# Up projections of two feed-forwards: seven half-size products a group in place of eight

## The chip, the cores and the metric

The kernel runs on 1 core of one Trainium2 chip. The metric is the device time of one execution in microseconds (us); the median of three runs of the kernel before is 2188.79 us (2188.71 to 2190.12). A time is compared with the kernel before on the same chip.

## The reference

A network of three layers over 256 tokens of 1024 channels, all in float32: two layers with a mixer, cross-attention to a memory and a gated feed-forward, then a layer with attention, a recurrence and 32 experts. The change lies in the two gated feed-forwards:

```python
def conv_glu_ffn(xn, w_up, conv_w, conv_b, w_down):
    u, gt = split_cols(xn @ w_up, (D_FF, D_FF))      # D_FF = 2752, w_up is 1024 x 5504
    u = causal_dwconv(u, conv_w, conv_b)             # 3 taps along the tokens
    return (jax.nn.silu(u) * gt) @ w_down
...
h = h + conv_glu_ffn(rms_norm(h, norm_ffn_g[layer]), ffn_w_up[layer], ffn_conv_w[layer],
                     ffn_conv_b[layer], ffn_w_down[layer])
```

## The kernel before

**Lanes.** The program is written once for each engine: a lane object (P for TensorE, V for VectorE, S for ScalarE, G for GpSimd, F for SyncE's DMA queue) issues in the order of the code. `mark` names the last instruction of a lane, `wait_ge` waits for such names. Each VectorE or ScalarE instruction also waits for the one before it on its engine. So each engine's order is written out by hand, and an instruction that waits holds all behind it.

**Layout.** Activations have channels on the 128 partitions and tokens on the free axis: `XT` is 8 blocks of 128 channels by 256 tokens. Weights are the stationary operand. `P.mm` (line 412 of the profile) on float32 shows in the profile as two LDWEIGHTS and two MATMUL. PSUM has 8 banks of 128 x 512; `P.tile` takes the next of banks 0 to 3, `P.occupy` a named one, and both wait until its last user is freed (`V.free`).

**Loads.** `LOADS` (line 195) is the order in which F issues the weight units of 2 MB into a ring of 4 slots of 4096 columns in feed-forward 0 and 5 in feed-forward 1 (line 591). A slot is loaded again once the unit in it was reported with `P.used`; at most 4 loads are in flight. Units `up0.g` and `up1.g` are the groups of the up projections, `dn` the down projection, `ada` the modulation weights that VectorE multiplies out behind each feed-forward.

**The feed-forward** (`ffn_p`, `ffn_s`, `ffn_v`, lines 2295 to 2390). The 2752 columns of u and of the gate are cut into 11 groups of 256 (the last has 192). For a full group TensorE fills two banks, one with u and one with the gate, each two tiles of 128 channels by 256 tokens, each tile 8 `mm` of 256 columns: 32 `mm` a group. In the last group the 64-wide tiles of u and gate are paired on the two halves of the array (`halves`). The rows that enter are not yet divided by their root mean square: ScalarE writes `XT` = gain x h and the squares as the layer before ends, TensorE adds the squares up after the first bank (`added_p`), ScalarE and VectorE make the root (`root_s`, `root_v`), which VectorE multiplies onto each bank as it takes it from PSUM. Then VectorE makes the causal convolution (per tile one multiply-add at line 323 and two at line 329), ScalarE the Silu, VectorE the product into `AC`, which the down projection reads. The down projection (`down_p`) adds 21 blocks and a half block into banks 4 to 7, in passes of 4 blocks, the last groups together in its last pass. Behind the last group VectorE works off the next mixer's small sums and the `ada` units beside the down projection.

```python
def added_p(P, n):
    b = P.tile(n + ".ss")
    P.wait_ge(f"{n}.qs")
    for c in range(2):
        P.mm(b[:, 0:256], ONESD, SQ[:, c, :], c == 0, c == 1, sig=n + ".ss" if c else None)
```

## Time and profile before

| | |
|---|---|
| median of 3 runs | 2188.79 us (2188.71 to 2190.12) |
| the profiled execution: own time, span | 2190.6 us, 2188.7 us |
| mean granted TensorE clock | 0.978 |
| busy: PE, PEld, DVE, ACT, POOL | 2057.1, 1372.6, 618.3, 367.0, 111.2 us |
| DMA | 587.77 MB, mean 269 GB/s |
| up projections of the two feed-forwards | from 359.34 and from 826.68 us after the span's start |

PE is TensorE's matmuls, PEld its weight loads, DVE VectorE, ACT ScalarE, POOL GpSimd, SPq the DMA queue of SyncE. A row of the timeline gives the start and the busy time in us, the engine, the line, the operation, output <- inputs with shapes, and xcount; in brackets the idle time before it and what ended it. Forms are rows by shape: busy us in all and mean ns of one.

### The profile page before, as it was taken

The page shows a single profiled execution, that of the slowest core. Times are in us where ns is not written, and L with a number is a line of the kernel's source. Part 1 is how long each engine was busy: PE and PEld are TensorE (multiplying, and loading weights), DVE is VectorE, ACT ScalarE, POOL GpSimd, SP SyncE. Part 2 cuts the span into 40 slices and gives each one's busy share as a digit, 9 for nine tenths or more (in the row PEclk, how much of TensorE's full clock was granted, in tenths as well). Part 3 has the DMA queues.
Part 4 walks back from the last instruction along what each step waited for, and adds up shares of the span by engine and source line. Part 5 has one row for each costly group of instructions (what it writes and reads, how often), then busy time and mean ns, then how long its engine had stood idle before and what let it go on. Part 6 is the DMA issues. An engine that isn't in the chain of part 4 may idle for free.

```text
span 2188.7 us, 27681 instructions
## 1 busy us (share of the span) xinstructions
PE 2057.1 (94%) x11650; PEld 1372.6 (63%) x11650; DVE 618.3 (28%) x1258; ACT 367.0 (17%) x706; POOL 111.2 (5%) x186
## 2 busy tenths in 40 slices
PE   9999999999999999999999999977699999898976
PEld 6888788888888888888777733322243333333423
DVE  5445432335364133344334321100011111101101
ACT  4322132000042121000232410100000100000101
POOL 0123100000000000000000000100000000001000
PEclk9999999999999999999999999988899999999987
DMA  7221343435524445348433499999999999999996
GB/s 269 107 78 41 155 174 116 154 144 222 212 82 154 154 163 220 141 159 332 174 132 130 183 381 426 427 427 427 427 426 411 427 427 427 427 427 428 420 427 283
DMA packets 44581, 587.77 MB, mean 269 GB/s; under 512 B 5393, under 2 KB 5665, under 8 KB 9505
## 3 DMA queue, kind: packets, MB, share of 16 engines
q1 hardware_dynamic: 44448, 585.92, 65.9%
q8 instruction: 94, 1.54, 0.3%
q14 instruction: 39, 0.31, 0.0%
HBM read 584.85 MB, written 1.05 MB: 268 GB/s over the span
## 4 chain that ended last, share of the span: by engine, by line
PE 69%; DMA 28%; ACT 1%; DVE 1%; issue 1%; SPq 0%; ACTq 0%; DVEq 0%
PE pb L412 68%; DMA ring<-in_gu 16%; DMA ring<-in_dne 9%; DMA arena<-in_dne 2%; PE pb L422 1%; DMA arena<-in_gu 1%; ACT arena L373 0%; DVE arena L329 0%; DMA xs<-in_rw_g 0%; DVE arena L323 0%; ACT arena L379 0%; SPq L591 0%; DVE ring L314 0%; DVE arena L314 0%; ACT xs L373 0%
## 5 line engine op out<-in xcount | busy, mean ns | idle before, releaser
L412 PE MATMUL pb<-arena,ring 128*128 128x256 f32 (+2 forms) x2784 | 605.8, 382 | 2.1 <-ACT arena L373 2.0
L412 PEld LDWEIGHTS pb<-arena,ring 128*128 128x128 f32 (+2 forms) x2784 | 519.1, 189 | 80.5 <-issue 7.5
L412 PE MATMUL pb<-arena 64*64 64x64 f32 (+12 forms) x3084 | 401.0, 342 | 19.8 <-DMA arena<-in_dne 10.5
L412 PEld LDWEIGHTS pb<-arena 64*64 64x64 f32 (+5 forms) x3084 | 280.9, 155 | 126.0 <-issue 94.1
L412 PE MATMUL pb<-arena,cst 128*64 128x512 f32 (+6 forms) x1108 | 275.4, 612 | 41.5 <-DMA ring<-in_gu 41.0
L412 PE MATMUL pb<-ring,cst 128*64 128x512 f32 (+2 forms) x784 | 246.9, 626 | 7.2 <-DMA arena<-in_gu 3.9
L412 PEld LDWEIGHTS pb<-arena,cst 128*64 128x64 f32 (+4 forms) x1108 | 88.8, 140 | 196.2 <-issue 193.9
L412 PE MATMUL pb<-ring,arena 128*64 128x512 f32 (+4 forms) x608 | 157.6, 536 | 8.0 <-DMA arena<-in_dne 6.3
L321 DVE TENSOR_SCALAR arena<-pb 128x512 f32<-128x512 f32 x30 | 20.7, 691 | 463.6 <-PE pb L412 463.6
L379 ACT ACTIVATE arena<-pb 128x512 f32<-128x512 f32 (+2 forms) x128 | 65.8, 514 | 490.2 <-PE pb L422 393.6
L373 ACT ACTIVATE arena<-arena 128x512 f32<-128x512 f32 (+6 forms) x151 | 87.7, 581 | 310.8 <-DVE arena L329 271.0
L314 DVE TENSOR_TENSOR arena<-pb,arena 128x512 f32<-128x512 f32 (+6 forms) x127 | 64.6, 509 | 223.6 <-PE pb L412 210.2
L412 PEld LDWEIGHTS pb<-ring,cst 128*64 128x64 f32 (+2 forms) x784 | 73.9, 139 | 77.1 <-issue 77.1
L323 DVE TENSOR_SCALAR arena<-pb 128x512 f32<-128x512 f32 x30 | 20.7, 691 | 333.6 <-PE pb L412 333.6
L412 PE MATMUL pb<-kv,cst 128*64 128x512 f32 (+2 forms) x240 | 110.6, 616 | 1.7 <-DMA ring<-in_gu 1.7
L412 PE MATMUL pb<-kv,arena 128*64 128x512 f32 (+4 forms) x288 | 95.4, 485 | 16.2 <-DMA arena<-in_dne 10.5
L412 PEld LDWEIGHTS pb<-ring,arena 128*64 128x64 f32 (+3 forms) x608 | 59.4, 140 | 55.9 <-issue 55.0
L314 DVE TENSOR_TENSOR arena<-arena 128x512 f32<-128x512 f32 (+6 forms) x134 | 79.0, 590 | 28.2 <-ACT arena L373 17.9
L379 ACT ACTIVATE memt<-pb 128x512 f32<-128x512 f32 (+1 forms) x39 | 22.0, 564 | 374.2 <-PE pb L412 374.0
L412 PE MATMUL pb<-arena,kv 128*128 128x256 f32 (+1 forms) x384 | 82.1, 381 | 1.2 <-ACT arena L379 1.2
L412 PEld LDWEIGHTS pb<-kv,arena 128*128 128x128 f32 (+2 forms) x288 | 42.7, 152 | 63.4 <-issue 61.9
L412 PEld LDWEIGHTS pb<-arena,kv 128*128 128x128 f32 (+1 forms) x384 | 68.8, 186 | 12.3 <-ACT arena L379 1.6
(149 smaller groups left out, 1479.8 us busy)
## 6 DMA issues: line engine op xcount, KB each, us to landing
arena<-in_gu SPq DMA_DIRECT2D x64, 2048.0 KB, 19.4
ring<-in_gu SPq DMA_DIRECT2D x49, 2048.0 KB, 19.4
arena<-in_dne SPq DMA_DIRECT2D x30, 2048.0 KB, 19.4
ring<-in_dne SPq DMA_DIRECT2D x22, 2048.0 KB, 19.4
kv<-in_gu SPq DMA_DIRECT2D x15, 2048.0 KB, 19.4
ring<-in_up SPq DMA_DIRECT2D x13, 2048.0 KB, 7.8
ring<-in_ada SPq DMA_DIRECT2D x8, 2048.0 KB, 7.8
kv<-in_dne SPq DMA_DIRECT2D x8, 2048.0 KB, 19.3
```

The lines of the kernel that those rows point to most:

```text
L314: self.e.tensor_tensor(out, a, b, op).then_inc(self.sem, 1)
L321: self.e.tensor_scalar(out, a, s1, None, op0).then_inc(self.sem, 1)
L323: self.e.tensor_scalar(out, a, s1, s2, op0, op1).then_inc(self.sem, 1)
L373: self.e.activation(out, a, func, bias=bias, scale=scale, accum_out=accum).then_inc(self.sem, 1)
L379: self.e.activation(out, a, ACT.Copy).then_inc(self.sem, 1)
L412: r = self.e.matmul(out, lhsT, rhs, start=start, stop=stop, skip_group_check=True)
L422: r = self.e.transpose(out, a, ident)
```

## The change

Each of the ten full groups of an up projection is a product of 2 x 2 blocks: the rows split in halves of tokens (i) and in even and odd channel blocks (e), `XA[i][e]`, the weights by e and by u or gate, `corners`. It is made with seven block products and sums (Winograd's form of Strassen's method) in place of eight. A block product is 8 `mm` of 128 columns into half a bank.

- The last, narrow group is done first, in the form that it had, on unscaled rows. Then VectorE scales the rows in place (`halved_v`) and makes four sums of them, once for each feed-forward.
- For each group VectorE makes four sums of weight blocks, 128 x 1024 elements each (`weight_sums_v`; t3 in place in the ring slot, the others in spare memory, two sets), in general one group ahead.
- TensorE runs P1, P6, P5, P7, P2, P4, P3 (`seven_p`); P2 is added onto P1 and P3 onto P5 in PSUM, after ScalarE has copied P1 out (`first`) and VectorE has read P5 (`c22`). In group 0 P2 comes second and has a bank of its own. Groups alternate between banks 0 to 3 and 4 to 7.
- VectorE combines: U2 = P1 + P6, U3 = U2 + P7, gate of the second tokens U3 + P5, u of them U3 - P4, gate of the first U2 + P5 + P3; u of the first is P1 + P2, copied by ScalarE. The convolution, Silu and product of a group are made while the next one is multiplied; its multiply with bias moves to ScalarE (`tap`).
- `LOADS` has the last group's unit first.

```diff
 LOADS = """
 ab_small ab.0 ab.1 ab.2 ab_r.1 ab_r.0 ab_r.2 rw_scratch wkv0.0 wkv0.1 wkv0.2 wkv0.3 mixo0.0 mixo0.1 wq0.0
-wq0.1 wo0.0 wo0.1 up0.0 up0.1 up0.2 up0.3 up0.4 up0.5 up0.6 up0.7 up0.8 up0.9 up0.10 dn0.0 ada.0 dn0.1 ada.1
+wq0.1 wo0.0 wo0.1 up0.10 up0.0 up0.1 up0.2 up0.3 up0.4 up0.5 up0.6 up0.7 up0.8 up0.9 dn0.0 ada.0 dn0.1 ada.1
...
-mixo1.1 wq1.0 wq1.1 wo1.0 ada.4 wo1.1 ada.5 up1.0 up1.1 up1.2 up1.3 up1.4 up1.5 up1.6 up1.7 up1.8 up1.9 up1.10
+mixo1.1 wq1.0 wq1.1 wo1.0 ada.4 wo1.1 ada.5 up1.10 up1.0 up1.1 up1.2 up1.3 up1.4 up1.5 up1.6 up1.7 up1.8 up1.9
...
+        XT4 = XT_.rearrange("p (q e t) -> p q e t", q=4, e=2)
+        XA = [[XT4[:, :, e, i * 128:(i + 1) * 128] for e in range(2)] for i in range(2)]
+        XSUM = MX_.rearrange("p (s q t) -> p s q t", s=4, q=4)
+        FIRST, U2, U3 = (XS_[:, o:o + 256].rearrange("p (j t) -> p j t", j=2) for o in (512, 768, 1024))
+        def corners(w):
+            q = w.rearrange("p (q e n) -> p q e n", q=4, e=2)
+            return [[q[:, :, e, h * 256:(h + 1) * 256] for h in range(2)] for e in range(2)]
+        def halved_v(V, n, after):
+            V.wait_ge(*after)
+            for i, e in ((0, 0), (0, 1), (1, 0), (1, 1)):
+                V.tt(XA[i][e], XA[i][e], bc(RB[:, i * 128:(i + 1) * 128], 1, 4), MUL)
+                V.mark(f"{n}.a{i}{e}")
+            s1, s2, s3, s4 = (XSUM[:, k] for k in range(4))
+            V.tt(s1, XA[1][0], XA[1][1], ADD)
+            V.tt(s2, s1, XA[0][0], SUB)
+            V.mark(f"{n}.s2")
+            V.tt(s3, XA[0][0], XA[1][0], SUB)
+            V.mark(f"{n}.s3")
+            V.tt(s4, XA[0][1], s2, SUB)
+            V.mark(f"{n}.s4")
+        def weight_sums_v(V, unit, spare, which, after=None):
+            b = corners(V.unit(unit)[:, 0:4096])
+            t1, t2, t4 = spare
+            if 1 in which:
+                if after is not None:
+                    V.wait_ge(after)
+                V.tt(t1, b[0][1], b[0][0], SUB)
+                V.tt(t2, b[1][1], t1, SUB)
+                V.mark(f"{unit}.t2")
+            if 3 in which:
+                V.tt(b[0][1], b[1][1], b[0][1], SUB)
+                V.mark(f"{unit}.t3")
+            if 4 in which:
+                V.tt(t4, t2, b[1][0], SUB)
+                V.mark(f"{unit}.t4")
+        def seven_p(P, unit, n, xn, spare, k0, first):
+            b = corners(P.unit(unit)[:, 0:4096])
+            t1, t2, t4 = spare
+            s1, s2, s3, s4 = (XSUM[:, k] for k in range(4))
+            def product(bank, lhs, rhs, sig, start=True):
+                for j in range(2):
+                    for q in range(4):
+                        P.mm(bank[:, j * 128:(j + 1) * 128], lhs[:, q, j * 128:(j + 1) * 128], rhs[:, q, :],
+                             start and j + q == 0, q == 3, sig=sig if (j, q) == (1, 3) else None)
+            one = P.occupy(f"{n}a", k0)
+            P.wait_ge(f"{xn}.a00")
+            product(one, b[0][0], XA[0][0], f"{n}.p1")
+            if first:
+                three = P.occupy(f"{n}f", 3)
+                P.wait_ge(f"{xn}.a01")
+                product(three, b[1][0], XA[0][1], f"{n}.p2")
+            six = P.occupy(f"{n}b", k0 + 1)
+            P.wait_ge(f"{xn}.s2", f"{unit}.t2")
+            product(six, t2, s2, f"{n}.p6")
+            five = P.occupy(f"{n}d", k0 + 2)
+            product(five, t1, s1, f"{n}.p5")
+            seven = P.occupy(f"{n}c", k0 + 3)
+            P.wait_ge(f"{xn}.s3", f"{unit}.t3")
+            product(seven, b[0][1], s3, f"{n}.p7")
+            if not first:
+                P.wait_ge(f"{n}.first")
+                product(one, b[1][0], XA[0][1], f"{n}.p2", start=False)
+            four = P.occupy(f"{n}e", k0 + 1)
+            P.wait_ge(f"{xn}.a11", f"{unit}.t4")
+            product(four, t4, XA[1][1], f"{n}.p4")
+            P.wait_ge(f"{xn}.s4", f"{n}.c22")
+            product(five, b[1][1], s4, f"{n}.p3", start=False)
             P.used(unit)
...
+        UG = XS_[:, 1536:2048].rearrange("p (q t) -> p q t", q=2)
+        SEVENS, LAST = 10, 10
+        quarter = lambda t, *at: [t[:, o:o + 1024].rearrange("p (q n) -> p q n", q=4) for o in at]
+        SPARE = [[quarter(KV_, 0, 1024, 2048), quarter(AR.t, 10752, 11776, 13312)],
+                 [quarter(AR.t, 8192, 9216, 10240), quarter(AR.t, 11264, 12288, 13312)]]
+        def first_bank(g):
+            return 4 - 4 * (g % 2)
         def ffn_p(P, n):
             P.begin(f"ffn{n}")
...
-            for g, (w2, tiles) in enumerate(FFN):
-                w = P.unit(f"up{n}.{g}")[:, 0:16 * w2].rearrange("p (k n) -> p k n", k=8)
-                names = [f"{f}.u{g}", f"{f}.g{g}"]
-                bs = [P.tile(name, hold=True) for name in names]
-                for b, name, c0 in zip(bs, names, (0, w2)):
-                    for q, (c1, cw) in enumerate(tiles):
-                        if cw < 128:
-                            if c0 == 0:
-                                halves(w, b, w2, c1, name)
-                            continue
-                        for c in range(8):
-                            P.wait_ge(f"{f}.x{c // 2}")
-                            P.mm(b[0:cw, q * 256:(q + 1) * 256], w[:, c, c0 + c1:c0 + c1 + cw], XT[:, c, :], c == 0,
-                                 c == 7, sig=name if (c == 7 and (q == 1 or (c0 and tiles[1][1] < 128))) else None)
-                    if g == 0 and c0 == 0:
...
+            w2, tiles = FFN[LAST]
+            P.main, P.i = [2], 0
+            w = P.unit(f"up{n}.{LAST}")[:, 0:16 * w2].rearrange("p (k n) -> p k n", k=8)
+            names = [f"{f}.u{LAST}", f"{f}.g{LAST}"]
+            for name, c0 in zip(names, (0, w2)):
+                b = P.occupy(name, 1 if c0 else 0)
+                for c in range(8):
+                    P.wait_ge(f"{f}.x{c // 2}")
+                    P.mm(b[:, 0:256], w[:, c, c0:c0 + 128], XT[:, c, :], c == 0, c == 7, sig=name if c0 and c == 7 else None)
+                if c0 == 0:
+                    halves(w, b, w2, 128, name)
+                    added_p(P, f)
+            P.used(f"up{n}.{LAST}")
+            for g in range(SEVENS):
+                seven_p(P, f"up{n}.{g}", f"{f}.{g}", f, SPARE[n][g % 2], first_bank(g), g == 0)
+            P.main, P.i = [0, 1, 2, 3], 0
             down_p(P, FBLOCKS, f"dn{n}", 4, f"dn{n}", ready=lambda kk: f"{f}.ac{kk}", merged=2,
                    halves=FHALF)
...
             root_s(S, f)
-            for g, (w2, tiles) in enumerate(FFN):
-                S.reach(f"{f}.g{g}")
-                cb = CB2[g % 2]
+            def tap(g):
+                S.wait_ge(f"{f}.u{g}.in")
+                for q, (c1, cw) in enumerate(FFN[g][1]):
...
+                    S.act(CB2[g % 2][0:cw, q, :], UB[0:cw, q, :], ACT.Identity,
...
+                S.mark(f"{f}.tap{g}")
+            def silu(g):
                 S.wait_ge(f"{f}.c{g}")
-                for q, (c1, cw) in enumerate(tiles):
-                    S.act(cb[0:cw, q, :], cb[0:cw, q, :], ACT.Silu)
+                for q, (c1, cw) in enumerate(FFN[g][1]):
+                    S.act(CB2[g % 2][0:cw, q, :], CB2[g % 2][0:cw, q, :], ACT.Silu)
                     S.mark(f"{f}.s{g}{q}")
+            def first(g):
+                S.wait_ge(f"{f}.{g}.p1")
+                if g:
+                    S.wait_ge(f"{f}.{g - 1}.u2" if g > 1 else f"{f}.0.c11")
+                S.copy(FIRST, tokens_half(S.banks[first_bank(g)]))
+                S.mark(f"{f}.{g}.first")
+            def copied(g):
+                S.wait_ge(f"{f}.{g}.p2", f"{f}.c{g - 1}")
+                S.copy(UB[:, :, 0:128], tokens_half(S.banks[first_bank(g)]))
+                S.free(f"{f}.{g}a")
+                S.mark(f"{f}.{g}.c11")
+            first(0)
+            S.free(f"{f}.0a")
+            tap(LAST)
+            silu(LAST)
+            tap(0)
+            for g in range(1, SEVENS):
+                first(g)
+                silu(g - 1)
+                copied(g)
+                tap(g)
+            silu(SEVENS - 1)
             S.table(LNEXP)
+            def conv(g):
+                V.wait_ge(f"{f}.tap{g}")
+                for q, (c1, cw) in enumerate(FFN[g][1]):
+                    cb, u = CB2[g % 2][0:cw, q, :], UB[0:cw, q, :]
+                    for k in (1, 0):
+                        o, late = coff["fcw"] + n * 66 + 22 * k + g * 2 + q, 2 - k
+                        V.stt(cb[:, late:256], u[:, 0:256 - late], COL[0:cw, o:o + 1], cb[:, late:256], MUL, ADD)
+                V.mark(f"{f}.c{g}")
+            def gated(g):
+                for q, (c1, cw) in enumerate(FFN[g][1]):
+                    V.wait_ge(f"{f}.s{g}{q}")
+                    cb, at = CB2[g % 2][0:cw, q, :], g * 2 + q
+                    V.tt(AC[0:cw, at, :], UG[0:cw, q, :], cb, MUL)
+                    if cw == 64:
+                        V.tt(AC[64:128, at, :], UG[0:cw, q, :], cb, MUL)
+                    V.mark(f"{f}.ac{at}")
+            def sums(g, *which):
+                if g < SEVENS:
+                    weight_sums_v(V, f"up{n}.{g}", SPARE[n][g % 2], which, f"used up{n}.{g - 2}" if g > 1 else None)
+            def last_in():
+                b = V.got(f"{f}.u{LAST}")
+                V.tt(UB[:, 0, :], b[:, 0:256], RB, MUL)
+                V.tt(UB[0:64, 1, :], b[0:64, 256:512], RB[0:64], MUL)
+                V.mark(f"{f}.u{LAST}.in")
+                V.tt(UG[0:64, 1, :], b[64:128, 256:512], RB[64:128], MUL)
+                V.free(f"{f}.u{LAST}")
+                b = V.got(f"{f}.g{LAST}")
+                V.tt(UG[:, 0, :], b[:, 0:256], RB, MUL)
+                V.free(f"{f}.g{LAST}")
             root_v(V, f)
...
+            sums(0, 1, 3, 4)
+            halved_v(V, f, (f"{f}.u{LAST}", f"{f}.g{LAST}"))
+            for g in range(SEVENS):
+                m, before = f"{f}.{g}", g - 1 if g else LAST
+                one, six, five, seven = (tokens_half(V.banks[first_bank(g) + k]) for k in range(4))
+                if g:
+                    sums(g + 1, 1)
+                V.wait_ge(f"{m}.first", f"{m}.p6")
+                V.tt(U2, FIRST, six, ADD)
+                V.mark(f"{m}.u2")
+                V.free(f"{m}b")
+                if g == 0:
+                    V.wait_ge(f"{m}.p2")
+                    last_in()
+                    sums(1, 1)
+                conv(before)
+                if g == 0:
+                    V.tt(UB[:, :, 0:128], FIRST, tokens_half(V.banks[3]), ADD)
+                    V.free(f"{m}f")
+                    V.mark(f"{m}.c11")
+                sums(g + 1, 3)
+                V.wait_ge(f"{m}.p7")
+                V.tt(U3, U2, seven, ADD)
+                V.free(f"{m}c")
+                gated(before)
+                V.wait_ge(f"{m}.p5")
+                V.tt(UG[:, :, 128:256], U3, five, ADD)
+                V.mark(f"{m}.c22")
+                sums(g + 1, 4)
+                V.wait_ge(f"{m}.p4")
+                if g:
+                    V.wait_ge(f"{m}.c11")
+                V.tt(UB[:, :, 128:256], U3, six, SUB)
+                V.free(f"{m}e")
+                V.mark(f"{f}.u{g}.in")
+                V.wait_ge(f"{m}.p3")
+                V.tt(UG[:, :, 0:128], U2, five, ADD)
+                V.free(f"{m}d")
+            conv(SEVENS - 1)
+            gated(SEVENS - 1)
...
                 if what in ("up0", "up1"):
-                    return [(0, 128, flat(what, 128, 16 * FFN[int(n)][0]))]
+                    at, size = (128 * 16 * sum(f[0] for f in FFN[k0:k1]) for k0, k1 in ((0, int(n)), (int(n), int(n) + 1)))
+                    return [(0, 128, dram[what][at:at + size].rearrange("(p n) -> p n", p=128))]
```

## Rows read from the trace of the kernel before

**Rows 1.** The page: chain that ended last by engine, and landing of loads.
```profile
PE 69%; DMA 28%; ACT 1%; DVE 1%; issue 1%; SPq 0%; ACTq 0%; DVEq 0%
...
ring<-in_up SPq DMA_DIRECT2D x13, 2048.0 KB, 7.8
```

**Rows 2.** The chain in order of time: start, length, what.
```profile
318.70 0.87 PE pb L422 x8
...
328.19 263.45 PE pb L412 x1240
...
795.52 259.14 PE pb L412 x1220
```

**Rows 3.** Stretches: both up projections, then one full group.
```profile
core 0: us, PE busy (x) PEld busy (x) DVE busy (x) ACT busy (x) POOL busy (x), PEclk, DMA share, GB/s
359.34:508.95 149.61, 149.61 (x709) 130.84 (x708) 57.04 (x115) 12.15 (x26) 0.00 (x0) 1.00 0.41 151
826.68:976.28 149.60, 149.60 (x709) 130.85 (x708) 57.04 (x115) 12.15 (x26) 0.00 (x0) 1.00 0.44 165
374.02:387.83 13.81, 13.81 (x65) 12.19 (x64) 4.99 (x10) 1.08 (x3) 0.00 (x0) 1.00 0.40 152
```

**Rows 4.** Timeline of PE in the expert part: 128 columns each, then what follows.
```profile
1283.03 3.74 PE L412 MATMUL pb<-arena,xs 128*128 128x128 f32 x32
1286.61 0.38 PE L422 MATMUL pb<-cst,arena 128*128 128x128 f32 x2
```

**Rows 5.** Timeline, feed-forward 0, weight loads of the last group: halves, then gate.
```profile
501.88 3.22 PEld L412 LDWEIGHTS pb<-arena,ring 128*64 128x64 f32 x32 [0.33 <-issue]
505.49 58.57 PEld L412 LDWEIGHTS pb<-arena,ring 128*128 128x128 f32 x272 [0.38 <-issue]
```

**Rows 6.** Timeline at the start of feed-forward 0.
```profile
359.34 7.07 PE L412 MATMUL pb<-arena 128*128 128x256 f32 x32
...
366.25 1.03 PE L412 MATMUL pb<-xs,small 128*128 128x256 f32 x4
...
367.31 0.47 ACT L373 ACTIVATE arena<-pb,small 128x256 f32<-128x256 f32 x1 [5.33 <-PE pb L412]
...
368.32 0.42 DVE L329 SCALAR_TENSOR_TENSOR arena<-pb,arena 128x256 f32<-128x256 f32 x1 [5.62 <-ACT arena L373]
...
369.70 0.69 DVE L314 TENSOR_TENSOR arena<-pb,arena 128x512 f32<-128x512 f32 x1
...
370.88 1.01 DVE L329 SCALAR_TENSOR_TENSOR arena<-arena,col 128x255 f32<-128x255 f32 x2
...
373.40 0.86 ACT L373 ACTIVATE arena<-arena 128x256 f32<-128x256 f32 x2 [3.81 <-DVE arena L329]
```

**Rows 7.** Timeline of DVE in two other places: sums of 1024 elements.
```profile
110.10 2.06 DVE L314 TENSOR_TENSOR arena<-arena 128x1024 f32<-128x1024 f32 x1
...
1148.00 3.75 DVE L314 TENSOR_TENSOR arena<-arena 128x1024 f32<-128x1024 f32 x3
```

**Rows 8.** Groups of DVE by form, whole span: 512 elements, 256 elements.
```profile
L314 DVE TENSOR_TENSOR arena<-arena 128x512 f32<-128x512 f32 x52 | 36.0, 692 | 4.4 <-DVE arena L329 0.5
...
L314 DVE TENSOR_TENSOR arena<-pb,arena 128x256 f32<-128x256 f32 x44 | 18.7, 425 | 31.7 <-PE pb L412 29.1
```

**Rows 9.** Stretches of 1 us around an idle PE, columns as in rows 3.
```profile
1057.00:1058.00 1.00, 0.31 (x2) 0.00 (x0) 0.93 (x3) 0.00 (x0) 0.00 (x0) 1.00 1.04 442
1058.00:1059.00 1.00, 0.00 (x0) 0.00 (x0) 0.93 (x3) 0.85 (x2) 0.00 (x0) 1.00 1.00 426
1059.00:1060.00 1.00, 0.69 (x3) 0.67 (x4) 0.93 (x3) 0.88 (x3) 0.00 (x0) 0.96 0.99 426
1060.00:1061.00 1.00, 1.00 (x4) 0.61 (x4) 0.93 (x3) 0.88 (x3) 0.00 (x0) 0.50 1.03 442
...
1063.00:1064.00 1.00, 1.00 (x5) 0.84 (x5) 0.30 (x1) 0.57 (x2) 0.00 (x0) 0.83 0.00 0
```

More of the change, by code:

```diff
@@ L831, in proj_tok_p @@
                          sig=f"{n}{i}" if c == 7 else None)
+            P.used(unit)
+        XT4 = XT_.rearrange("p (q e t) -> p q e t", q=4, e=2)
[5 more added lines that the diff above has]
+            return [[q[:, :, e, h * 256:(h + 1) * 256] for h in range(2)] for e in range(2)]
@@ new lines, in tokens_half @@
+        def tokens_half(bank):
+            return bank[:, 0:256].rearrange("p (j t) -> p j t", j=2)
+        def seven_p(P, unit, n, xn, spare, k0, first):
[30 more added lines that the diff above has]
+            product(five, b[1][1], s4, f"{n}.p3", start=False)
@@ L2304, in halves @@
                          sig=name if c == 7 else None)
-            for g, (w2, tiles) in enumerate(FFN):
-                w = P.unit(f"up{n}.{g}")[:, 0:16 * w2].rearrange("p (k n) -> p k n", k=8)
-                names = [f"{f}.u{g}", f"{f}.g{g}"]
-                bs = [P.tile(name, hold=True) for name in names]
-                for b, name, c0 in zip(bs, names, (0, w2)):
-                    for q, (c1, cw) in enumerate(tiles):
-                        if cw < 128:
-                            if c0 == 0:
-                                halves(w, b, w2, c1, name)
-                            continue
-                        for c in range(8):
-                            P.wait_ge(f"{f}.x{c // 2}")
-                            P.mm(b[0:cw, q * 256:(q + 1) * 256], w[:, c, c0 + c1:c0 + c1 + cw], XT[:, c, :], c == 0,
-                                 c == 7, sig=name if (c == 7 and (q == 1 or (c0 and tiles[1][1] < 128))) else None)
-                    if g == 0 and c0 == 0:
-                        added_p(P, f)
-                P.used(f"up{n}.{g}")
-                for name in names:
-                    P.release(name)
+            w2, tiles = FFN[LAST]
[14 more added lines that the diff above has]
+            P.main, P.i = [0, 1, 2, 3], 0
             down_p(P, FBLOCKS, f"dn{n}", 4, f"dn{n}", ready=lambda kk: f"{f}.ac{kk}", merged=2,
@@ L2347, in ffn_v @@
             added_v(V, f)
-            root_v(V, f)
-            def fc(name, at, cw):
-                o = coff[name] + at
-                return COL[0:cw, o:o + 1]
-            def normed(b, tiles):
-                if len(tiles) == 2 and tiles[1][1] == 128:
-                    V.tt(UB, pair(b), bc(RB, 1, 2), MUL)
-                else:
-                    for q, (c1, cw) in enumerate(tiles):
-                        V.tt(UB[0:cw, q, :], b[0:cw, q * 256:(q + 1) * 256], RB[0:cw], MUL)
-            for g, (w2, tiles) in enumerate(FFN):
-                cb = CB2[g % 2]
-                ub = [UB[0:cw, q, :] for q, (_, cw) in enumerate(tiles)]
-                b = V.tile(f"{f}.u{g}")
-                normed(b, tiles)
-                if tiles[1][1] == 64:
-                    ub[1] = CB2[1 - g % 2][0:64, 1, :]
-                    V.tt(ub[1], b[64:128, 256:512], RB[64:128], MUL)
-                V.free(f"{f}.u{g}")
-                for q, (c1, cw) in enumerate(tiles):
-                    jj = g * 2 + q
-                    conv_v(V, cb[0:cw, q, :], UB[0:cw, q, :],
-                           [fc("fcw", n * 66 + 22 * k + jj, cw) for k in range(3)], fc("fcb", n * 22 + jj, cw))
-                V.mark(f"{f}.c{g}")
-                normed(V.tile(f"{f}.g{g}"), [t for t in tiles if t[1] == 128])
-                V.free(f"{f}.g{g}")
-                for q, (c1, cw) in enumerate(tiles):
-                    V.wait_ge(f"{f}.s{g}{q}")
-                    V.tt(AC[0:cw, g * 2 + q, :], ub[q], cb[0:cw, q, :], MUL)
-                    if cw == 64:
-                        V.tt(AC[64:128, g * 2 + q, :], ub[q], cb[0:cw, q, :], MUL)
-                    V.mark(f"{f}.ac{g * 2 + q}")
```

4 lines of the change are left out of this document (added).

## The prediction

> **What bounds the kernel.** I read the page's chain first: TensorE (PE) makes 69% of it, the DMA engines 28% [rows 1]. Then the chain in order of time, to see which share the two feed-forwards have: each lies inside one unbroken PE piece of about 260 us [rows 2], so neither loads nor other engines end a wait there, and a microsecond of PE saved there, or of PE idleness added, moves everything behind it, the loads of the expert part too, as their slots are freed by PE. Then the stretches of the up projections: 149.6 us each, PE busy for all of it at granted clock 1.00, VectorE (DVE) for 57.0, ScalarE (ACT) for 12.2, GpSimd for nothing, and a full group costs 13.81 us [rows 3]. The kernel's `mm` on f32 shows as two MATMULs, so a group's 32 products are 64 instructions of 0.2158 us. DVE has 8.8 us to spare in each group. The question is what the new order asks of DVE, and when.
>
> **Removed and added on PE.** A full group becomes seven products of 8 `mm` with 128 columns in place of 32 with 256: 7 x 16 = 112 MATMULs. Columns fall to 7/8, but each instruction is only 128 columns long and each takes new weights. The nearest rows: 32 such matmuls start at 1283.03 and the next at 1286.61, 0.1119 us each; runs of 8 transposes of the same shape take 0.87 us, 0.1088 each [rows 4]. I take 0.1117, since a product stream is long like the first: 1.79 us a product, 12.51 a group, 1.30 less than before. Ten groups and two feed-forwards: **-26.0 us**; at 0.1088 it would be 32.5. (The Trainium skill, TensorE: Matmul & The Clock Gate, "Wait — 56ns, not 53.3ns?", gives a fixed 2.5 ns per matmul over the column time. The 0.2158 us here agree, taken as two passes; for 128 columns that makes an estimate of 0.1092, so the gain would be 5.6 us more; the long run says 0.0025 more per instruction.)
>
> **The last group goes first**, on unscaled rows, with bank and work unchanged: first product 3.45 us, the halves 3.61 (501.88 to 505.49 [rows 5]), the sum of squares 0.86, gates 3.45. It only moves, at no cost.
>
> **First new wait: rows and weight sums before group 0.** At feed-forward 0, PE starts at 359.34 [rows 6]. The sum of squares is then issued by 359.34 + 3.45 + 3.61 = 366.40 (before: 366.25), and PE ends the last group at 366.40 + 0.86 + 3.45 = 370.7. DVE has the root at 369.70 + 0.15 = 369.85 [rows 6]. Its queue then holds the four weight sums of group 0 (`sums(0, 1, 3, 4)`, 1024 elements each): three such operations take 3.75 us in a row [rows 7], 1.26 each with the gap, so 5.04, until 374.9. Only then come the scaled rows, 512 elements each: 0.69 [rows 8], until 375.6, and PE begins P1 at about 375.65. **PE idle 5.0 us.** P1 and P2 (3.6 us) then just cover the other three scalings and s1, s2 (5 x 0.73 = 3.65): 0.1 us more.
>
> **Second new wait: C22 of group 0.** P6, P5, P7, P4 follow, until 375.65 + 6 x 1.79 + 0.1 = 386.45. P3 adds into the bank of P5, so it waits for `c22`. DVE gets P6 at 381.3 and has these ahead of `c22`, in its own order: U2 (256 elements from PSUM, 0.425 [rows 8], 0.465 with the gap), the four of `last_in` 1.85, `sums(1,1)` 2.52, the convolution of the last group 2.08 (1.01 for two of four [rows 6]), C11 0.46, `sums(1,3)` 1.26, U3 0.46, three of `gated` 1.4, C22 0.42: 10.9 us, until 392.3. ACT's Silu (0.86 for two [rows 6]) fits beside `sums(1,3)`. **PE idle 5.9 us.** P3 ends at 394.1.
>
> **Steady state.** From group 1 the weight sums run a group ahead. Count from PE's start of a group: DVE ends the last UG of the group before at 0.7, `sums(g+1,1)` at 3.2, waits for P6 (3.57 + 0.2), U2 at 4.25, the convolution at 6.3, `sums(g+1,3)` at 7.6, U3 at 8.1, `gated` at 9.0, C22 at 9.5. PE reaches P3 at 10.7: covered with 1.2 us over. The fourth sum ends at 10.75, before P4 is done (10.9). DVE is busy 10.4 of 12.5 us (4 x 1.26, 5 + 2 of 0.465, 2.08). Loads: a slot is filled again a group's length after it is free, and a load of `up` lands 7.8 us after its issue [rows 1]; DVE asks for a group's weights one group sooner than PE did, still about 25 us after the issue. Cost nothing, in all three. The units that follow `up` are asked for one place later in the ring, 2 MB in 12.5 us. The last scalar table, Silu and tail of DVE lie behind the down projection, whose first passes need only early groups.
>
> Without the clock, one up projection: 11.4 (last group and sum) + 4.95 + 10.8 + 5.85 + 1.8 + 9 x 12.51 = 147.4 against 11.4 + 10 x 13.81 = 149.5 us, twice: **-4.2 us**.
>
> **The clock.** The nearest idle stretch of PE is the one at 1057.3 to 1059.3, 2.0 us: then the granted clock was 0.50 for about 3.4 us of work (1060 to 1063.4) and 1.00 again [rows 9]. At 0.50 (1.2 in place of 2.4 GHz) that costs half of 3.4 us, 1.7. My idle stretches are longer (5.0, 5.9), so each should bring it; part of the slow stretch may fall into the idle one, and it can come twice. Bounds per wait: 0 and 3.4; I take 1.5, near the one row. Four waits: **+6.0 us**. In the first pair it delays P6 and with it `c22`, so nothing hides it. (The Trainium skill, the same page, "Loop structure matters more than you think": long waits between bursts of matmuls take the clock back to its lower level. The row at 1060 agrees. By that rule all four waits pay, by the -4.2 alone none does.)
>
> **Sum**: -26.0 + 21.8 (both waits and the 0.1, twice) + 6.0 = +1.8 us. The profiled execution took 2190.6 us, 1.8 more than the median 2188.8; I add the change to the median: **2190.6**. Under 0.2% (4.4 us) a measurement here can't tell from no change.
>
> **The rivals.**
> (1) *The PE stream is faster than I take it, or the clock stays up.* 0.1088 us per matmul gives 2190.6 - 6.5 = 2184.1; with no clock drop as well, 2178. For it: the 8-runs [rows 4]. Against: the 32-run, and the row of the clock. By the Trainium skill's figure alone, in place of 0.1117, it would be 2185.0.
> (2) *Slower: VectorE's `c22` comes late in every group.* Place: P3's wait; slack 1.2 us. Ahead of it stand three sums and nine smaller operations since the wait at the group's start, so it decides once they take 0.1 us more each. A 128x1024 sum did take 2.06 us where GpSimd worked beside it [rows 7]: three at +0.8 less the slack are 1.2 us, in 18 groups 22 us, so 2212; half of that, 2201. Against: GpSimd does nothing in these stretches [rows 3].
> (3) *Slower: the half clock comes twice after each wait*, 3.4 us each: -4.2 + 13.6 gives 2198.2. The row shows it once after 2.0 us; nothing shows it for 5 to 6.
> (4) The change doesn't give the seventh it names: this is in my sum (1.30 of 13.81 us, 9%, not 12.5%).
>
> **Chances.** Forecast 0.55; (1) 0.17; (2) 0.13; (3) 0.15. All of the forecast's own range, 2186.5 to 2193, is within 0.2%; (1) is faster, (2) and (3) slower. The range goes from 2181.5 (most of 1) to 2201 (3 and the mild form of 2).
>
> **What would show it.** Two PE idle stretches per feed-forward, released by VectorE, of about 5.0 us (before the first 128-column product) and 5.9 (ahead of the seventh product of group 0), and none after; clock rows of 0.50 behind each; groups of 12.5 us by windows; each up projection 147.4 us plus the clock's part, 150 to 151; 128x1024 sums at 1.23 us; nothing changed in length after 509 or before 359. Wrong if a PE wait recurs in each group, if groups take 12.2 us, or if the idle stretches are shorter since the sums are not in the way.

## The result, and the profile after

| | before | after |
|---|---|---|
| median | 2188.75 us (2188.64 to 2190.12, 4 runs) | 2205.33 us (2204.82 to 2207.88, 4 runs) |
| the profiled execution: own time, span | 2190.6 us, 2188.7 us | 2205.69 us, 2203.9 us |
| mean granted TensorE clock | 0.978 | 0.971 |
| first up projection, from the span's start | 359.34 to 508.95 us | 370.95 to 523.15 us |
| second up projection | 826.68 to 976.28 us | 840.95 to 993.88 us |

The ratio is 1.0076, 95% interval 1.0064 to 1.0088: 16.6 us slower by the medians, 15.2 by the two spans. The forecast was 2190.6, at most 2201.0.

First the page of after, the chain that ended last; it answers to [rows 1].

```profile
PE 67%; DMA 28%; DVE 3%; ACT 1%; issue 1%; SPq 0%; DVEq 0%; ACTq 0%
PE pb L412 66%; DMA ring<-in_gu 9%; DMA kv<-in_gu 6%; DMA kv<-in_dne 4%; DMA ring<-in_dne 3%; DMA arena<-in_gu 3%; DMA arena<-in_dne 2%; DVE arena L314 1%; PE pb L422 1%; ACT arena L373 1%; DVE arena L329 1%; DMA arena<-in_cond 0%; DMA xs<-in_rw_g 0%; DVE ring L314 0%; DVE kv L314 0%
```

VectorE's share rose from 1 to 3%, and there is a link that the chain before did not have: a load of `in_cond`. Nothing in the up projections reads it.

The stretches of after: both up projections, then a steady group; columns as in [rows 3], to which they answer.

```profile
370.95:523.15 152.20, 141.24 (x1189) 138.11 (x1188) 109.52 (x170) 32.56 (x67) 0.00 (x0) 0.97 0.41 153
840.95:993.88 152.93, 141.97 (x1189) 138.84 (x1188) 109.54 (x170) 32.53 (x67) 0.00 (x0) 0.96 0.45 169
423.10:435.61 12.51, 12.51 (x115) 12.51 (x113) 9.78 (x15) 2.81 (x7) 0.00 (x0) 1.00 0.45 170
```

A group takes 12.51 us, as forecast to the hundredth; PE idles for 10.96 us in each up projection (152.20 - 141.24), and the clock is under 1.00 in both. Yet these stretches hold only 2.59 + 3.33 = 5.9 of the 15.2 us. The first begins 11.61 us late, so most of the loss lies **ahead** of the changed code. From the end of the second to the end of the span after needs 1210.0 us, 2.4 less than before, in code that wasn't touched. 11.61 + 2.59 + 0.07 (between the two) + 3.33 - 2.4 = 15.2.

SyncE's own timeline in after, ahead of feed-forward 0 (start, length, line, load):

```profile
273.74 14.14 SPq L591 DMA_DIRECT2D ring<-in_wo  x2
302.23 0.33 SPq L591 DMA_DIRECT2D arena<-in_up  x1
302.61 0.42 SPq L600 DMA_DIRECT2D arena<-in_cond  x1
```

and the same place before:

```profile
272.97 14.14 SPq L591 DMA_DIRECT2D ring<-in_wo  x2
287.16 0.42 SPq L600 DMA_DIRECT2D arena<-in_cond  x1
...
301.46 0.33 SPq L591 DMA_DIRECT2D arena<-in_up  x1
```

Before, the small load of `cond` was issued at 287.16, ahead of the first `up` unit, which then waited on the queue for its ring slot until 301.46. After, the two stand the other way round, and `cond` is issued at 302.61. SyncE's lane says why: its fetches are tied to a unit by name, and that unit is no longer the first of its kind.

```python
for name in LOADS.split():
    ...
    if name == "up0.0":
        F.wait_ge("mixo0.a3")
        F.get("cond", CROW, dram["cond"].partition_broadcast(128))
        ...
    F.load(name, *block(name))
```

Who waits for it, in the timeline of after, all engines (in brackets the idle time and what ended it):

```profile
310.60 3.23 ACT L373 ACTIVATE arena<-arena 128x1024 f32<-128x1024 f32 x3 [14.34 <-DMA arena<-in_cond]
313.86 1.22 DVE L314 TENSOR_TENSOR arena<-arena 128x1024 f32<-128x1024 f32 x1 [16.17 <-ACT arena L373]
...
316.75 6.65 PE L412 MATMUL pb<-kv,arena 128*128 128x256 f32 x16 [7.64 <-DVE arena L314]
```

and the stretch at the half clock (granted 0.50, that is 1.2 GHz in place of 2.4), columns as in [rows 3]:

```profile
312.50:322.80 10.30, 6.05 (x14) 4.88 (x15) 4.16 (x6) 2.42 (x6) 0.00 (x0) 0.50 0.00 0
```

ScalarE waits 14.34 us for `cond`, VectorE for ScalarE, and VectorE's next work is what TensorE's attention scores need. Before, the same ScalarE work started at 295.78 after a wait of 0.30 us, and the scores at 308.17. They now come 8.58 us later; 0.77 of this is older (SyncE was already 0.77 late at 273.74, and the last section has the wait that made it), so 7.8, and half of the 6.05 us of matmuls at the half clock is 3.0 more: **10.8 us** before feed-forward 0 starts.

Then the two forecast waits, in the timeline of after, PE and DVE:

```profile
381.73 1.23 DVE L314 TENSOR_TENSOR kv<-ring 128x1024 f32<-128x1024 f32 x1
382.99 1.23 DVE L314 TENSOR_TENSOR kv<-ring,kv 128x1024 f32<-128x1024 f32 x1
384.25 1.23 DVE L314 TENSOR_TENSOR ring<-ring 128x1024 f32<-128x1024 f32 x1
385.51 1.23 DVE L314 TENSOR_TENSOR kv<-kv,ring 128x1024 f32<-128x1024 f32 x1
386.84 5.77 DVE L314 TENSOR_TENSOR arena<-arena 128x512 f32<-128x512 f32 x8
387.68 5.40 PE L412 MATMUL pb<-arena,ring 128*128 128x128 f32 x32 [4.99 <-DVE arena L314]
...
406.19 6.35 PE L412 MATMUL pb<-arena,ring 128*128 128x128 f32 x32 [5.96 <-DVE xs L314]
```

Four weight sums, then the rows, and PE has idled 4.99 us; then 5.96 us for `c22`. Feed-forward 1 shows 4.99 and 5.97, and no other PE wait of an up projection stands in the trace. The 32 matmuls behind each wait take 5.40 and 6.35 us where others take 3.74: the half clock. In the stretches behind the waits it is:

```profile
388.00:389.00 1.00, 1.00 (x6) 1.00 (x6) 0.95 (x2) 0.00 (x0) 0.00 (x0) 0.50 1.03 442
...
405.00:407.00 2.00, 0.81 (x4) 0.81 (x5) 1.90 (x4) 0.00 (x0) 0.00 (x0) 0.50 0.00 0
407.00:409.00 2.00, 2.00 (x11) 2.00 (x11) 0.81 (x2) 1.01 (x2) 0.00 (x0) 0.50 0.03 8
409.00:411.00 2.00, 2.00 (x11) 2.00 (x11) 0.89 (x2) 0.19 (x1) 0.00 (x0) 0.50 0.17 33
```

It lasts from 387.6 to 391.0 and from 404.7 to 411.5, in feed-forward 1 from 855.2 to 862.1 and from 875.7 to 882.5. The matmul work in the four is 3.3, 5.3, 4.5 and 5.9 us; half of it is lost: 1.65 + 2.65 + 2.25 + 2.95 = **9.5 us** in place of the 6.0 of the forecast.

### The profile page after: what moved, and what is told of

The parts are those of the page before. It is cut to its first block, busy times and chain, and to the rows that moved or that the text cites. A ratio compares the mean times of both kernels' runs of the same rounds, so it can differ in the third digit from the quotient of the medians.

```text
span 2203.9 us, 29905 instructions
## 1 busy us (share of the span) xinstructions
PE 2043.0 (93%) x12610; PEld 1388.1 (63%) x12610; DVE 724.4 (33%) x1372; ACT 408.0 (19%) x788; POOL 111.2 (5%) x186
## 3 DMA queue, kind: packets, MB, share of 16 engines
q8 instruction: 101, 1.65, 0.3%
## 4 chain that ended last, share of the span: by engine, by line
PE 67%; DMA 28%; DVE 3%; ACT 1%; issue 1%; SPq 0%; DVEq 0%; ACTq 0%
PE pb L412 66%; DMA ring<-in_gu 9%; DMA kv<-in_gu 6%; DMA kv<-in_dne 4%; DMA ring<-in_dne 3%; DMA arena<-in_gu 3%; DMA arena<-in_dne 2%; DVE arena L314 1%; PE pb L422 1%; ACT arena L373 1%; DVE arena L329 1%; DMA arena<-in_cond 0%; DMA xs<-in_rw_g 0%; DVE ring L314 0%; DVE kv L314 0%
## 5 line engine op out<-in xcount | busy, mean ns | idle before, releaser
L412 PE MATMUL pb<-arena,ring 128*128 128x256 f32 (+3 forms) x2816 | 527.8, 350 | 13.1 <-DVE xs L314 6.0
L412 PEld LDWEIGHTS pb<-arena,ring 128*128 128x128 f32 (+2 forms) x2816 | 461.9, 192 | 70.8 <-issue 12.6
L412 PE MATMUL pb<-arena 128*128 128x128 f32 (+14 forms) x3804 | 454.3, 322 | 19.4 <-DMA arena<-in_dne 10.3
L412 PEld LDWEIGHTS pb<-arena 128*128 128x128 f32 (+5 forms) x3804 | 340.2, 162 | 118.4 <-issue 92.6
L412 PE MATMUL pb<-ring,cst 128*64 128x512 f32 (+2 forms) x784 | 247.4, 625 | 10.2 <-DMA arena<-in_gu 3.9
L373 ACT ACTIVATE arena<-arena 128x512 f32<-128x512 f32 (+5 forms) x151 | 87.7, 581 | 145.2 <-DVE arena L329 90.9
L412 PE MATMUL pb<-arena,kv 128*128 128x128 f32 (+2 forms) x592 | 97.8, 325 | 12.1 <-DVE xs L314 6.0
L314 DVE TENSOR_TENSOR arena<-arena 128x512 f32<-128x512 f32 (+5 forms) x120 | 90.2, 751 | 39.4 <-ACT arena L373 32.6
L412 PEld LDWEIGHTS pb<-arena,kv 128*128 128x128 f32 (+1 forms) x592 | 86.8, 200 | 18.8 <-DVE xs L314 6.2
L412 PE MATMUL pb<-memt,arena 128*128 128x512 f32 (+3 forms) x204 | 70.6, 504 | 1.2 <-ACT memt L379 1.2
L314 DVE TENSOR_TENSOR ht<-pb,ht 128x512 f32<-128x512 f32 x24 | 16.6, 691 | 163.6 <-PE pb L412 163.6
```

Source lines behind the costliest of these rows:

```text
L314: self.e.tensor_tensor(out, a, b, op).then_inc(self.sem, 1)
L373: self.e.activation(out, a, func, bias=bias, scale=scale, accum_out=accum).then_inc(self.sem, 1)
L412: r = self.e.matmul(out, lhsT, rhs, start=start, stop=stop, skip_group_check=True)
```

## The experiments

Each is compared with the kernel before on the same chip; a median is one of 4 to 10 runs.

**The load's place alone.** e1_cond_first is after with the fetches ahead of the first `up` unit again; e2_before_cond_late is the kernel before with only the fetches moved behind its first `up` unit.

```diff
 # e1, on after
-                if name == "up0.0":
+                if name == "up0.10":
 # e2, on before
-                if name == "up0.0":
+                if name == "up0.1":
```

> The changed kernel with one line different: the DMA queue fetches the condition vector and the gate weights ahead of up0.10 (as it did ahead of up0.0 before the change), not behind it. Theory (queue): up0.10 waits on SyncE for its ring slot until about 302 us, cond is issued 15 us later than before, ScalarE stands before it in cross-attention 0 and PE with it; with the line moved, cond is issued near 287 us again, the PE idle stretch of 7.6 us and the half clock of 10.2 us behind it go, feed-forward 0 starts near 359 to 360 us, and the time falls by 10.8 us from 2205.3 to about 2194.5. Rival (the loss lies elsewhere, in the ring's rotation or the clock): the idle stretch before feed-forward 0 stays or comes back in another place, and the time stays within 3 us of 2205.

> The kernel before, with nothing of the seven products: only cond and the gate weights are fetched behind the first up unit in place of ahead of it. Theory (queue): the same idle stretch of 7 to 8 us before the keys' scores of cross-attention 0, half clock behind it, +10.8 us: 2188.8 to about 2199.6. Rival (the wait belongs to the new products or to the new order of groups): no change, 2188.8.

Measured: e1 2196.04 us (2193.62 to 2197.34), ratio 1.0028 [1.0017, 1.0039]; e2 2199.49 us (2198.8 to 2201.26), ratio 1.0046 [1.003, 1.0063]. The timeline of PE in e2, a kernel without any of the seven products, and its half clock (columns as in [rows 3]):

```profile
317.06 5.45 PE L412 MATMUL pb<-kv,arena 128*128 128x256 f32 x16 [8.47 <-DVE arena L314]
```
```profile
313.80:320.60 6.80, 3.54 (x8) 2.86 (x9) 3.30 (x4) 0.34 (x1) 0.00 (x0) 0.50 0.00 0
```

8.47 + 3.54 / 2 = 10.2 us, and the median rose by 9.9 against the runs of before beside it. In e1 there is no PE wait there, and the loss against before falls from 16.6 to 6.4 us (2196.04 - 2189.62), so by 10.2. The order of two loads is worth 10 us and the rest of the change 6.4: shown from both sides. The stretch of feed-forward 1, where the edit touches nothing, is 152.90 us in e1 and was 152.93 in after.

**The clock apart from the waits.** e5_warm_in_waits is e1 with TensorE kept at work in its two waits, on products that nobody reads; VectorE's order, and so the time at which PE may go on, is unchanged.

```diff
+            if first:
+                for _ in range(11):
+                    P.mm(one[:, 256:512], ident, cst["tri"], True, True)
             P.wait_ge(f"{xn}.a00")
...
+            if first:
+                idle = P.occupy(f"{n}w", 2)
+                for _ in range(13):
+                    P.mm(idle[:, 256:512], ident, cst["tri"], True, True)
+                P.free(f"{n}w")
             P.wait_ge(f"{xn}.s4", f"{n}.c22")
```

> e1 with 11 and 13 matmuls of 256 columns whose result nobody reads, put ahead of PE's two waits of group 0 in each feed-forward (4.7 and 5.6 us of work in waits of 5.0 and 6.0). Theory (the clock's price is what the -4.2 us lack): the granted clock stays at 1.00 through both up projections, each is about 147.5 us long, and the time falls from 2194.5 by about 9.5 us to 2185. Rival (half clock costs nothing that isn't in the waits already, something else makes the up projections 152 to 153 us): 2194 or more.

Measured: 2187.87 us (2184.58 to 2191.52, 10 runs), ratio 0.9991 [0.9981, 1.0]. Feed-forward 1 in e1 and in e5, stretches with columns as in [rows 3]:

```profile
828.67:981.57 152.90, 141.94 (x1189) 138.82 (x1188) 109.55 (x170) 32.56 (x67) 0.00 (x0) 0.96 0.45 170
```
```profile
827.67:975.81 148.14, 147.64 (x1237) 143.04 (x1236) 109.54 (x170) 32.58 (x67) 0.00 (x0) 1.00 0.47 175
```

The waits are filled, nothing is computed sooner, and the up projection is 4.76 us shorter at a clock of 1.00. By the medians the clock behind four waits was worth 8.2 us, where 9.5 were expected. The time came out 2.9 above what was expected, 1.5 of it because e1 itself lay that much above its own; 10 runs spread over 6.9 us, and the profiled one lost 3 us before the changed code (the last section shows where).

**The first wait.** e3_sums_early is e1 with the weight sums of group 0 ahead of the root, in a gap of VectorE.

```diff
-            root_v(V, f)
-            sums(0, 1, 3, 4)
+            sums(0, 1, 3, 4)
+            root_v(V, f)
```

> e1 with the four weight sums of group 0 issued on VectorE before the root, where VectorE stands idle for 5.6 us, not behind it. Theory (VectorE's order makes the first wait): the idle stretch of 4.99 us falls to about 0.9 us in each feed-forward (root at 369.9, last group's PE done at 370.9 in the old count, scaling 0.7), the half clock behind it goes too (1.7 to 2.3 us each): 2194.5 to about 2182.5. The second wait stays at 5.9 to 6.0. Rival (the wait is for the scaled rows or the load of up0.0, not for the sums): 4 us or more of idle stay, 2194.

Measured: 2182.29 us (2181.65 to 2183.81), ratio 0.9966 [0.9954, 0.9979]. The timeline of PE in e3, feed-forward 0:

```profile
372.02 3.81 PE L412 MATMUL pb<-arena,ring 128*128 128x128 f32 x32 [0.88 <-DVE arena L314]
...
389.00 5.43 PE L412 MATMUL pb<-arena,ring 128*128 128x128 f32 x32 [5.97 <-DVE xs L314]
```

The first wait shrank from 4.99 to 0.88 us and no half clock follows it (3.81 us for 32 matmuls); the second stayed at 5.97 with its half clock. One line moved turned a kernel 6.4 us slower than before into one 7.3 us faster, 13.8 us where 12 were expected.

**The slack at `c22`.** The forecast had 1.2 us of it in a steady group, from a count of VectorE's queue. e7_two_more_sums is e1 with the first sum of each group computed three times over: 2.5 us more of VectorE work ahead of `c22`.

```diff
-                V.tt(t1, b[0][1], b[0][0], SUB)
+                for _ in range(3):
+                    V.tt(t1, b[0][1], b[0][0], SUB)
```

> e1 with the first weight sum of every group made three times over, 2 x 1.26 us more on VectorE ahead of c22, results unchanged. Theory (steady state has 1.2 us of slack at c22, and PE alone paces it): each of groups 1 to 8 shows a new PE idle stretch of about 1.3 us and lasts 13.8 us in place of 12.51; the two waits of group 0 grow by 2.5 us each: per feed-forward 10.4 + 5.0 us, from 2196.0 to about 2227, up to 2232 with more half clock behind the longer waits. Rival A (VectorE has 2.1 us free in 12.5 wherever it falls, so only 0.4 us a group is lost): groups of 12.9 us, 2212. Rival B (no slack now): groups of 15 us, 2247.

Measured: 2222.81 us (2221.11 to 2223.85), ratio 1.0153 [1.0135, 1.0172]. The timeline of PE in e7: both waits of group 0, then those of groups 1 to 3.

```profile
378.04 6.56 PE L412 MATMUL pb<-arena,ring 128*128 128x128 f32 x32 [7.51 <-DVE arena L314]
...
400.23 5.77 PE L412 MATMUL pb<-arena,ring 128*128 128x128 f32 x32 [8.48 <-DVE xs L314]
...
415.55 3.84 PE L412 MATMUL pb<-arena,ring 128*128 128x128 f32 x32 [0.62 <-DVE xs L314]
...
429.15 2.05 PE L412 MATMUL pb<-arena,ring 128*128 128x128 f32 x16 [0.83 <-DVE xs L314]
...
442.75 2.05 PE L412 MATMUL pb<-arena 128*128 128x128 f32 x16 [0.83 <-DVE xs L314]
```

Now a wait recurs in each of the groups 1 to 8: 0.62 us in the first, then 0.83. From P3 to P3 a group takes 13.60 us (429.15 to 442.75), 1.09 more than 12.51, where the theory had 13.8. How much slack there was stands in the steady group of after that begins at 423.10, in the timelines of DVE (U2, then `c22`) and of PE (P3):

```profile
426.93 0.42 DVE L314 TENSOR_TENSOR xs<-xs,pb 128x256 f32<-128x256 f32 x1 [0.62 <-PE pb L412]
...
432.30 0.42 DVE L314 TENSOR_TENSOR xs<-xs,pb 128x256 f32<-128x256 f32 x1
```
```profile
433.82 1.95 PE L412 MATMUL pb<-arena,ring 128*128 128x128 f32 x16
```

`c22` is done at 432.72 and P3 begins at 433.82: 1.1 us of slack, so the count of 1.2 was right. But VectorE also waits 0.62 us for P6 ahead of U2, and in e7 that wait is gone. Of the 2.52 us of added work it takes 0.62 and the slack 1.10; 0.8 is left, and PE waits 0.83. The recorded count has this wait for P6 too (from 3.2 to 3.77 us), but the theory of e7 left it out. Rival 2 was real as a mechanism and 1.7 us of VectorE work away.

**The second wait, two ways.** e4_group0_order is e3 with VectorE's order in group 0 changed: the last group's rows are taken in before U2, and the sums of group 1 stand behind `c22`. e6_sums_ahead puts the sums of group 0 ahead of the residual of cross-attention, those of group 1 ahead of the root, and keeps the last group's gate in `AC`, so that `c22` need not wait for that group's convolution, Silu and product.

```diff
 # e4, group 0
+                    last_in()
                 V.wait_ge(f"{m}.first", f"{m}.p6")
...
-                    sums(1, 1)
...
-                sums(g + 1, 3)
+                if g:
+                    sums(g + 1, 3)
...
                 V.mark(f"{m}.c22")
-                sums(g + 1, 4)
+                if g:
+                    sums(g + 1, 4)
...
+                if g == 0:
+                    sums(1, 1, 3)
 # e6
+            V.wait_ge(f"{x}.o3")
+            weight_sums_v(V, f"up{n}.0", SPARE[n][0], (1, 3, 4))
             residual_v(V, f"wo{n}")
...
+            sums(1, 1, 3, 4)
             root_v(V, f)
-            sums(0, 1, 3, 4)
...
-                V.tt(UG[:, 0, :], b[:, 0:256], RB, MUL)
+                V.tt(AC[:, 20, :], b[:, 0:256], RB, MUL)
```

> e3 with VectorE's order in group 0 changed: the last group's intake (last_in) comes while P6 runs, and the weight sums of group 1 (sums 1, 3, 4) come behind c22, not ahead of it. Theory (c22 waits for what stands ahead of it in VectorE's queue): the second idle stretch falls from 5.96 to about 1.6 us; the sums put off come back as one stretch of about 1.5 us ahead of P3 of group 1; the half clock behind the second wait (1.7 and 2.2 us in e3) goes. Per feed-forward 2.9 + 1.95 us: from 2182.3 to about 2172.6. Rival (P3 waits for the PSUM bank or for P5's sum itself, not for the queue): the stretch stays at 6 us and the time at 2182.

> The version that should beat both: e1 with the weight sums of group 0 made before the residual of cross-attention, where VectorE waits 22.8 us for PE, those of group 1 before the root, and the last group's gate kept in its own place (AC) so that c22 need not wait for the last group's convolution, Silu and product. Theory: one idle stretch of 0.9 us per feed-forward is left (last group's end to the scaled rows), none at c22, granted clock 1.00, each up projection 137.5 to 138 us against 149.6: 24 us under the kernel before, about 2165.5 beside 2189.6. Rival (VectorE's work of 10.4 us in 12.5 has no room for the backlog at the start, stretches come back in group 1 or 2): 2170 or more.

Measured: e4 2175.8 us (2173.01 to 2179.8), ratio 0.9943 [0.9925, 0.9961]; e6 2175.04 us (2173.82 to 2178.49), ratio 0.9938 [0.992, 0.9956]. e4 has waits of 0.88, 1.44 and 1.91 us in each up projection, and the clock stays at 1.00 through all (141.68 us, feed-forward 1). e6 missed its 2165.5 by 9.5 us. Its feed-forward 0 was nearly as meant (138.4 us, with one wait of 0.34 in group 1); most of the loss stands ahead of feed-forward 1, in the timeline of e6, all engines:

```profile
811.85 1.22 DVE L314 TENSOR_TENSOR arena<-kv 128x1024 f32<-128x1024 f32 x1 [20.54 <-DMA kv<-in_up]
...
816.96 3.08 DVE L314 TENSOR_TENSOR ht<-pb,ht 128x512 f32<-128x512 f32 x4
817.68 1.05 ACT L373 ACTIVATE arena<-ht,col 128x256 f32<-128x256 f32 x2 [30.51 <-DVE ht L314]
...
818.87 4.64 PE L412 MATMUL pb<-arena,ring 128*128 128x256 f32 x12 [4.71 <-ACT arena L373]
...
824.19 4.73 PE L412 MATMUL pb<-arena,ring 128*128 128x256 f32 x36 [0.67 <-ACT arena L373]
```

VectorE waited 20.54 us for the load of `up1.0`, with the residual queued behind it, and PE lost 4.71 and 0.67 us, with 3.4 us at the half clock (818.4 to 821.8) behind the first. It is a queue's order again: an instruction moved ahead on its engine to where its load is not there yet holds all behind it.

**Both put together.** e8_sums_behind_c22 is e6 without the early sums in feed-forward 1, and with the weight sums of the next group behind `c22` in every group.

```diff
-            weight_sums_v(V, f"up{n}.0", SPARE[n][0], (1, 3, 4))
+            if n == 0:
+                weight_sums_v(V, f"up{n}.0", SPARE[n][0], (1, 3, 4))
...
-            sums(1, 1, 3, 4)
+            sums(n ^ 1, 1, 3, 4)
             root_v(V, f)
...
                 V.mark(f"{m}.c22")
+                if g or n:
+                    sums(g + 1, 1)
```

(turns 3 and 4 of the sums follow the mark of u and the last UG in the same way; their places ahead of `c22` go.)

> The run e6_sums_ahead with two edits. In feed-forward 1 no weight sum stands ahead of the residual any more (there VectorE was late for the next load and PE waited 4.71 and 0.67 us, with 3.4 us at the half clock behind them); the sums of group 0 stand ahead of the root and those of group 1 behind c22. And in every group the three turns of weight sums for the next group stand behind c22 instead of ahead of it. Theory (every wait left in e6 is VectorE's order): 2175.0 - 4.7 - 0.7 - 1.7 - 0.7 (the 0.34 of group 1, twice) = 2167.3 us; feed-forward 1 begins near 814.7 without a wait ahead of it, each up projection takes 138.0 us, groups 12.51 us each, the granted clock is 1.00 throughout both. Rival 1 (the sums now come late for the next group: t3 or t4 ends 1.8 us into it, and P6 or P7 waits for them): a PE wait of 0.5 to 1 us recurs in each group, 2175 to 2185 us. Rival 2 (the sums of group 1 are late in feed-forward 1 alone, as in e4_group0_order): 2 to 3.4 us more there, 2169.5 to 2171.

Measured: **2167.07 us** (2165.61 to 2168.12, 4 runs), ratio 0.99 [0.9884, 0.9917] against 2189.45 us for before: 22.4 us faster. Both up projections, stretches of e8:

```profile
359.18:497.19 138.01, 137.13 (x1190) 134.21 (x1189) 104.67 (x167) 32.66 (x67) 0.00 (x0) 1.00 0.45 168
813.00:952.68 139.68, 137.44 (x1189) 134.16 (x1188) 109.58 (x170) 32.55 (x67) 0.00 (x0) 1.00 0.50 185
```

The first is what was expected, 138.0; in the second rival 2 of that run holds in a mild form, PE waits of 0.60 and 0.77 us for group 1's sums and `c22`. The total still met the theory because the second began at 813.0, not at 814.7. Against 149.6 us before, 21.5 us are gained here, of the 26.0 that the products alone bring. Between the two up projections this profiled execution is another 1.9 us shorter than before's (315.8 against 317.7), most of which is not the change's doing: before's has 3.4 us of half clock there, in code that is the same in both, and this one has none (the last section).

## Why the prediction was wrong

**The step that failed** stands under "Steady state": the loads were to "Cost nothing, in all three", and the last part staked "nothing changed in length after 509 or before 359". I asked when each unit is asked for and whether its slot is free; I did not ask what else is in SyncE's lane between the units, and so left this queue at nothing. The unit moved to the front of `LOADS` passed the fetches of `cond` and the gates, whose place hangs on the name `up0.0`, and SyncE held them for 14.7 us (302.61 - 287.16, less the 0.77) while it waited for a slot. Worth 10.8 us in the trace of after; 10.2 in the trace of e2 and 9.9 by its medians; 10.2 by e1. Without it the loss is the 6.4 us of e1, and the time would have been inside the range.

**The clock term was too small.** 1.5 us a wait came from a half clock of 3.4 us behind an idle stretch of 2.0 [rows 9]. Behind 5 to 6 us it lasted 3.4 once and 6.8 to 6.9 three times, of which 1.65 to 2.95 us were lost: 9.5 in place of 6.0. The mechanism was right, and e5 shows it apart from the waits. The row that the 1.5 rested on was weaker than it looked: the same wait of 2.00 us stands in all ten traces, and the half clock followed it in six. Rival 3, at 0.15, was nearly the case: its second stretch of half clock came behind three of the four waits, and it had 13.6 us, what it costs if all of each stretch holds work. (The Trainium skill, TensorE: Matmul & The Clock Gate, "Loop structure matters more than you think", has long waits between bursts of matmuls take the clock back to its lower level. All four waits here did so.)

**Right, as forecast:** 12.51 us a group, 0.1117 us a matmul; waits of 5.0 and 5.9 (4.99 and 5.96), their places and their releaser; 1.23 us a sum; no wait in a steady group, with a slack of 1.1 us where 1.2 were counted. Without the clock an up projection takes 152.20 - 4.3 = 147.9 and 152.93 - 5.2 = 147.7 us against the 147.4 forecast; most of the 0.4 (twice) is the last group and its sum of squares, 11.7 in place of 11.4 us (370.95 to 382.69). Rival 1 (a faster stream) is out: the 128-column stream runs at the rate of the 32-run in [rows 4], not of the short runs of 8 (whose 0.87 us stands in [rows 2]; the forecast names [rows 4] for it). (The Trainium skill, TensorE: Matmul & The Clock Gate, "Wait — 56ns, not 53.3ns?", gives 2.5 ns per matmul over the column time. Counted once for each instruction, that was my estimate of 0.1092. The trace shows 0.1117, 12.51 / 112, and decides.) Rival 4, the seventh as 9%, is the measured group.

**The sum** on the profiled spans: +1.8 forecast, + 10.8 for the load, + 3.5 for the clock, + 0.6 for the rest of the stretches (5.92 measured against the 1.8 and the 3.5), + 0.8 ahead of the load and between the two feed-forwards, - 2.4 behind the second, is 15.1, against 15.2 measured. Nothing shows that the - 2.4 is the change's doing: from the end of the wait of [rows 9] to the end of the span, in code that no run touches, the ten traces take 1127.1 (after) to 1129.6 us, and before 1129.4. The 1.4 by which the medians' 16.6 stand above the 15.2 lies in which executions were profiled: that of before was 1.8 us above its median, that of after 0.4.

## What to carry to other kernels

When a list of loads is reordered, read the DMA lane's whole program and not the list alone: a small fetch tied to a unit's name moves with it, behind a slot wait of many microseconds, and the price falls due where no code was changed. Price a new wait on TensorE with the half clock behind it (17 of 17 times behind 4.7 us and more here, six of ten behind 2.0), and look first whether the work ahead of it is needed at all at that point: here one line moved was worth 14 us. What stood ahead of what in two queues, VectorE's and SyncE's, made products that save 26 us into a loss of 16.6; with both orders mended the same products gave 22.4. Work moved forward to fill a gap needs its own inputs there; else it holds the queue (e6).
